# Expert order by rank, transposed network outputs and reordered norms in a two-block transformer kernel

## The reference

```python
proj = rms_norm(x, norm1_g) @ w_in              # 1024 x 3600
mq, mk, mv, mo, mi, mf, aq, ak, av = split(proj)
qk = silu(conv5(concat([mq, mk])))              # centred depthwise convolution over tokens
y_m = gated mLSTM of qk, mv, mo, mi, mf, both directions
y_a = dilated attention of rope(aq), rope(ak), av
x = x + concat([y_m, y_a]) @ w_out
u = relu(rms_norm(x, norm2_g) @ w_up)           # 1024 x 4096
x = x + (u * u) @ w_down
```

```python
x = layer_norm(ALPHA * x + h)                   # l0, l2
logits = x @ router                             # 8 experts, the best 2 of each token
for e in range(8):
    y = y + combine[:, e:e+1] * ((silu(g) * u) @ w_down[e])   # g, u = split(x @ w_gu[e]), 3584 wide
x = layer_norm(ALPHA * x + y)                   # l1, l3
```

## Time and profile before

| | |
|---|---|
| median of three runs | 2263.12 us |
| the profiled execution | 2262.86 us |
| its span, first to last instruction | 2261.0 us |
| PE, DVE, ACT busy share of the span | 95%, 71%, 58% |

### The profile page before, as it was taken

How to read it: one execution, slowest core, us unless ns; L and a number is a source line. 1 busy time by engine, 2 the same in 40 slices (tenths; PEclk the granted TensorE clock), 3 DMA queues, 4 the chain that set the end, 5 groups by cost and what they waited for, 6 DMA issues and landing times.

```text
span 2261.0 us, 26000 instructions
## 1 busy us (share of the span) xinstructions
PE 2140.9 (95%) x10012; PEld 1723.4 (76%) x10012; DVE 1601.9 (71%) x1566; ACT 1319.2 (58%) x1378; POOL 20.4 (1%) x32
## 2 busy tenths in 40 slices
PE   8889999989999999999888999999999999999997
PEld 7767887767888788877667888788888877777775
DVE  5866555776555645566756555788888899999998
ACT  6454444644544443444544544576776788888876
POOL 0000000000000000000000000000000000000000
PEclk9999999999999999997899999999999999999999
DMA  6314443422654345442007554789898999999995
GB/s 265 140 47 172 187 186 132 177 94 75 251 186 185 141 182 191 159 144 75 1 19 280 205 218 180 271 343 350 331 372 331 365 361 421 390 421 377 421 383 247
DMA packets 74625, 524.29 MB, mean 232 GB/s; under 512 B 8736, under 2 KB 9184, under 8 KB 12160
## 3 DMA queue, kind: packets, MB, share of 16 engines
q1 hardware_dynamic: 71712, 511.64, 58.5%
q0 software_dynamic: 2784, 10.93, 1.4%
HBM read 521.48 MB, written 1.05 MB: 231 GB/s over the span
## 4 chain that ended last, share of the span: by engine, by line
PE 68%; DVE 19%; issue 5%; ACT 5%; DMA 3%; DVEq 0%; SPq 0%; ACTq 0%
PE psum L518 58%; DVE LO L509 10%; DMA ring<-in_experts 2%; ACT HI L501 2%; DVE AR L1585 1%; PE psum L1055 1%; PE psum L2460 1%; PE psum L904 1%; PE psum L1050 1%; PE psum L841 1%; PE psum L686 1%; PE psum L667 1%; PE psum L1977 1%; PE psum L2523 1%; DVE AR L858 1%
## 5 line engine op out<-in xcount | busy, mean ns | idle before, releaser
L509 DVE TENSOR_TENSOR LO<-ring,HI 128x2048 fp32r<-128x2048 f32 x379 | 850.5, 2258 | 391.1 <-ACT HI L501 388.9
L501 ACT ACTIVATE HI<-ring 128x2048 fp32r<-128x2048 f32 x379 | 712.7, 1887 | 350.7 <-PE psum L518 339.5
L518 PE MATMUL psum<-HI,XT 128*128 128x512 f32 (+1 forms) x3152 | 803.9, 393 | 20.1 <-issue 5.1
L518 PEld LDWEIGHTS psum<-HI,XT 128*128 128x128 f32 x3152 | 592.0, 191 | 162.6 <-DVE XT L702 10.6
L518 PE MATMUL psum<-LO,XT 128*128 128x512 f32 (+1 forms) x1856 | 507.5, 395 | 17.1 <-DVE LO L509 14.6
L518 PEld LDWEIGHTS psum<-LO,XT 128*128 128x128 f32 x1856 | 345.6, 190 | 112.7 <-DVE LO L509 44.5
L518 PE MATMUL psum<-HI,HTH 128*128 128x512 f32 x848 | 305.4, 401 | 6.8 <-DVE HTH L1107 6.8
L509 DVE TENSOR_TENSOR LO<-AR,HI 128x2048 fp32r<-128x2048 f32 x112 | 254.7, 2289 | 53.5 <-ACT HI L501 52.9
L501 ACT ACTIVATE HI<-AR 128x2048 fp32r<-128x2048 f32 x112 | 212.5, 1910 | 59.0 <-PE psum L518 57.1
L518 PE MATMUL psum<-LO,HTH 128*128 128x512 f32 x848 | 229.1, 392 | 0.0
L518 PE MATMUL psum<-HI,HTL 128*128 128x512 f32 x568 | 221.5, 390 | 0.0
(11 more groups left out here) (281 smaller groups left out, 1462.8 us busy)
## 6 DMA issues: line engine op xcount, KB each, us to landing
ring<-in_experts SPq DMA_DIRECT2D x224, 1024.0 KB, 6.7
ring<-in_dense SPq DMA_DIRECT2D x149, 1024.0 KB, 4.8
AR<-in_experts SPq DMA_DIRECT2D x112, 1024.0 KB, 6.9
bcs<-in_ln_g POOLq DMA_DIRECT2D x4, 512.0 KB, 4.5
bcs<-in_ln_b POOLq DMA_DIRECT2D x4, 512.0 KB, 5.1
bcs<-in_norm_g POOLq DMA_DIRECT2D x3, 512.0 KB, 3.9
cons<-in_cons POOLq DMA_DIRECT2D x1, 1317.0 KB, 8.0
X<-in_x SPq DMA_DIRECT2D x2, 512.0 KB, 3.9
```

The costliest lines, as they stand in the source:

```text
L501: e.activation(HI[:, h:h + m], slot(u), ACT.Copy).then_inc(*high.up(u))
L509: e.tensor_tensor(LO[:, h:h + m], slot(u), HI[:, h:h + m].bitcast(F32), ALU.subtract).then_inc(*low.up(u))
L518: ins = e.matmul(out_ap, lhsT=a, rhs=b, start=start and n == 0, stop=stop and n == len(pairs) - 1)
```

## The change

Five things change. First, `SEATS` puts the experts in the order of ranks 0, 4, 1, 5, 2, 6, 3, 7; the tables KINDS, `thr` and the permutation follow it. Second, in ff0 and ff1 the chunks 1 to 7 are made transposed by `across`: the weights of the array are 128 columns of the unit, and the 256 tokens stream through. So the 8 transposes of such a chunk are gone, and ACT and DVE make HTH and HTL from SBUF. Third, part 1 (mk) of the front is made by `across` too, its transposes and its first eviction are gone. Fourth, in l2 `cols_lo` of tile 0 comes after the centred rows of tile 1. Fifth, in l3 the sum, mean and centring of tile 1 come before the last rows of tile 0.

```diff
+SEATS = [0, 4, 1, 5, 2, 6, 3, 7]
...
+    limits = [192.5, 128.5, 128.5, 999.0, 64.5, 64.5, 64.5, 999.0]
+    add("thr", np.tile(np.array(limits)[SEATS], (P, 1)))
+    add("seats", np.tile(np.array(SEATS), (P, 1)))
...
+        def across(e, use, key, x_ready):
+            for b in range(2):
+                banks.take(e, *use, b)
+            n = units[place[(*key, 0)]][0]
+            us = next_units(e, (*key, 0), KB // n)
+            for i, u in enumerate(us):
+                hv, lv = hi_lo(u)
+                last = i == len(us) - 1
+                for t in range(2):
+                    for w in x_ready(t, n * (i + 1) - 1):
+                        e.wait_ge(*w)
+                e.wait_ge(*high.of(u))
+                for b in range(2):
+                    for j in range(2):
+                        products(e, banks.get(*use, b)[:, j * S:j * S + S],
+                                 [(hv[:, k, tile(b * 2 + j)], z[:, i * n + k, :]) for k in range(n)
+                                  for z in (XTH, XTL)], i == 0 and j == 0, False)
+                e.wait_ge(*low.of(u))
+                for b in range(2):
+                    for j in range(2):
+                        ins = products(e, banks.get(*use, b)[:, j * S:j * S + S],
+                                       [(lv[:, k, tile(b * 2 + j)], XTH[:, i * n + k, :])
+                                        for k in range(n)], False, last and j == 1)
...
+        def still(c, gated):
+
+            return c >= 1 and not gated
+
         def net_up_tensor(e, use, key, c, kinds, gated, ready, swap, tile1=None):
+            if still(c, gated):
+                return across(e, (use, "up", c), (key, "up", c), ready)
...
+            if still(c, gated):
+                for b in range(2):
+                    e.wait_ge(*v_done.of(use, "gate", c, b))
+                    if c >= 2:
+                        e.wait_ge(*filled.of(use, "downed", c - 2))
+                    e.wait_ge(*a_order.last)
+                    e.activation(HTH[:, hb, 2 * b:2 * b + 2, :],
+                                 GS[:, hb, b, :].rearrange("p (j s) -> p j s", j=2),
+                                 ACT.Copy).then_inc(*a_done.up(use, "turn", c, b))
+                return between()
...
-            cols(e, ("raw", l, 1), ("qk", l, 1), BOTH, xr)
+            across(e, ("raw", l, 1), ("qk", l, 1), xr)
             few(e, ("gates", l), ("gates", l), xr)
-            pad_tensor(e, l, 0)
+            pad_tensor(e, l)
             cols(e, ("mv", l), ("mv", l), BOTH, xr,
                  mid={0: lambda: few_turn(e, ("gates", l), ("gates", l))})
-            pad_tensor(e, l, 1)
...
-                evict(e, ("raw", l, 1), t, raw[1][:, t, :])
+            pad_across(e, l)
...
-            pad_scalar(e, l, 1)
...
+        KINDS = [[kinds[r] for r in SEATS] for kinds in KINDS]
+        WIDTH = [[sum(kind) for kind in kinds] for kinds in KINDS]
...
-            e.tensor_tensor(PERM, bc3(RANK, 8, 1), bc3(idx, 8, 2), ALU.is_equal).then_inc(*v_done.up())
+            e.tensor_tensor(PERM, bc3(RANK, 8, 1), bc3(C("seats"), 8, 2),
+                            ALU.is_equal).then_inc(*v_done.up())
...
-                ln_apply(e, "l2", t, *vector("l2"), *vector("l2b"))
-                if t == 0:
+                ln_mean(e, "l2", t)
+                ln_center(e, t, *vector("l2"))
+                if t:
                     cols_lo(e, "l2", 0)
+                ln_sum(e, "l2", t)
+                ln_rows(e, "l2", t, *vector("l2b"))
...
-                ln_apply(e, "l3", t, *vector("l3"), *vector("l3b"))
+                ln_mean(e, "l3", t)
+                if t:
+                    ln_sum(e, "l3", 0)
+                ln_center(e, t, *vector("l3"))
+            for t in range(2):
+                if t == 0:
+                    ln_sum(e, "l3", 1)
+                ln_rows(e, "l3", t, *vector("l3b"))
```

More of the change, by code:

```diff
@@ L577, in cols_by_tile @@
                     between()
+        def across(e, use, key, x_ready):
[21 more added lines that the diff above has]
+                                        for k in range(n)], False, last and j == 1)
+                    if b:
+                        ins.then_inc(*used.up(u))
+                        if last:
+                            filled.tell((*use, b), used, u)
+                    elif last:
+                        ins.then_inc(*filled.up(*use, b))
         def row_part(e, use, t, u, i, kb, hb, first, stop, kinds, h_ready):
@@ L1010, in net_up_scalar @@
                 if c >= 2:
-                    e.wait_ge(*filled.of(use, "turn", c - 2, len(kinds) - 1))
+                    if still(c - 2, gated):
+                        e.wait_ge(*v_done.of(use, "turn", c - 2, t))
+                    else:
+                        e.wait_ge(*filled.of(use, "turn", c - 2, len(kinds) - 1))
                 e.wait_ge(*a_order.last)
@@ L1056, in net_turn_tensor, with net_turn_scalar @@
                 ins.then_inc(*filled.up(use, "turn", c, t))
[L1058 removed]
+        def net_turn_scalar(e, use, c, n, kinds, between, gated=True):
             hb, nb = c % 2, n // P
+            if still(c, gated):
+                for b in range(2):
[7 more added lines that the diff above has]
+                return between()
             for t, kind in enumerate(kinds):
@@ L1082, in net_turn_scalar, with net_turn_vector @@
                              ACT.Copy).then_inc(*a_done.up(use, "turn", c, t))
-        def net_turn_vector(e, use, c, n, kinds, between):
+        def net_turn_vector(e, use, c, n, kinds, between, gated=True):
             hb, nb = c % 2, n // P
+            if still(c, gated):
+                for b in range(2):
+                    xh = HTH[:, hb, 2 * b:2 * b + 2, :]
+                    e.wait_ge(*a_done.of(use, "turn", c, b))
+                    e.wait_ge(*v_order.last)
+                    e.tensor_tensor(HTL[:, hb, 2 * b:2 * b + 2, :],
+                                    GS[:, hb, b, :].rearrange("p (j s) -> p j s", j=2),
+                                    xh.bitcast(F32), ALU.subtract).then_inc(
+                        *v_done.up(use, "turn", c, b))
+                return between()
             for t, kind in enumerate(kinds):
@@ L1108, in net_turn_vector, with net_down_tensor @@
                                 ALU.subtract).then_inc(*v_done.up(use, "low", c, t))
-        def net_down_tensor(e, use, key, c, last, acc, kinds):
-            ready = [(v_bank if kind == P else v_done).of(use, "turn" if kind == P else "low", c, t)
-                     for t, kind in enumerate(kinds)]
+        def net_down_tensor(e, use, key, c, last, acc, kinds, gated):
+            ready = [(v_done if still(c, gated) or kind != P else v_bank).of(
+                use, "turn" if kind == P else "low", c, t) for t, kind in enumerate(kinds)]
             n = 0
```

85 lines of the change are left out of this document (56 added, 29 removed).

## The result

The changed kernel takes 2267.72 us (median of 19 runs, 2262.98 to 2276.85) against 2263.45 us (19 runs, 2258.34 to 2273.44) for the kernel before: ratio 1.0024, 95% interval 1.0013 to 1.0035. The forecast was 2250.5 us, with a range of 2243.5 to 2258.5. So the kernel is slower by 0.24%: the interval leaves out 1, but the change is smaller than the 0.5% that the prediction took as the least that can be told from no change. The median is 9 us beyond the range. Of the rivals only the third and fourth pointed up, and neither happened.

What follows compares the result with a forecast made beforehand. PE was taken to bound most of the kernel, the HI and LO chain the light experts, with DMA close behind. Terms -6.5 - 3.8 + 1.2 - 1.8 - 0.5 - 1.0 = -12.4 us gave 2250.5 us, range 2243.5 to 2258.5.

Steps and rivals of the forecast that it cites:

- third: Rival: in the networks and fronts, weight loads of 191 ns bound PE with 256-column matmuls; about 2359 us, chance 0.02.
- fourth: Rival: the limits meet the wrong ranks in the new expert order, so the other side runs; about 2528 us, chance 0.01.
- The order, -6.5 forecast: Experts: light ones all following heavy ones give -8.4, dearer fetches +1.5, heavy ones +0.4; between -8.4 and 0 us.
- 2.8 us a light expert: Experts: a light one after a heavy one takes 108.0 us, after a light one mean 110.8; three more gain 8.4.
- the sixth unit: Heavy experts: PE needs it at about 13.6 us; DVE ends its LO at 12.9 after heavy, 12.1 after light.
- the dearer fetch: Light experts: three now fetch 128 tokens for the next instead of 64, which costs 1.5 us back on DVE.
- the low end, nothing: Heavy experts following light ones: lower bound of their added cost, nothing; high end 6.9 us, 0.4 us taken.
- The networks, -3.8: ff0 and ff1: removed transposes give -12.5 us, 256-column matmuls cost +8.7; net -3.8 us.
- The fronts, +1.2: Front of each layer: part 1 by across costs PE +0.62 us, removed transposes give nothing; between -0.5 and +1.5.
- l2, -1.8 and -0.5: Norm l2: tile 1's last rows start 1.8 us earlier; the shorter PE gap gives the router's clock another 0.5 us.
- l3, -1.0: Norm l3: with tile 1's centring before tile 0's last rows, the end comes at 2257.5 us, -1.0 us.
- the signs that the prediction named as wrong: Profile: a heavy expert over 129 us, light ones still at 111, or pairs of matmuls away from 0.120.

Runs made afterwards that it cites:

- old places: The changed kernel with par at 232 columns instead of 144, so later tensors keep the addresses of the kernel before: 2254.18 us, ratio 0.9974.
- all but the order: The changed kernel with the old order of experts and the tensor addresses of the kernel before (par 232): 2255.52 us, ratio 0.9975.
- before again: The kernel before, unchanged, run once more for a trace: 2258.96 us in a single run.
- AR moved: The kernel before with EPS declared behind AR, so TMP2, TG and AR move by 32 bytes: 2255.99 us in a single run.
- order alone: The kernel before with only the new order of experts, tensors at the addresses of before (par 232): 2256.72 us, ratio 0.9981.
- right LO moved: Changed kernel at old places; in light experts' last turn but one, DVE makes the hidden rows' low part before LO: 2248.02 us, ratio 0.9934.

## Why the prediction was wrong

**The step that failed** is the price of the matmuls that don't change. The prediction took 0.227 us for 512 columns from the earlier trace rows, and by adding up its steps on the time of before it kept that pace for the changed kernel: the move of the tensors has no term in the sum, which puts it at nothing, without a reason. With XT, HTH and HTL moved by 352 bytes, the pace of 512 columns in the dense layers is 0.233. At one clock that costs 16.9 us, more than all that the change gains there (8.9): the kernel after is 7.8 us slower than before (2265.3 against some 2257.5). -12.4 + 16.9 would be +4.5 us, beside the 4.3 us measured between the medians. That closeness is luck: the real gain at old places was 8.9 us and not 12.4, and the 19 runs of before, of which only one has its clock on record, have a median of 2263.45 us, where its other sets have 2259.28 to 2262.36.

The same 0.227 was a misreading for the heavy experts. The prediction made 2.72 us of it for a unit; with XT it is 12 x 0.233 = 2.80, and the sixth unit is wanted at 14.0 us and not 13.6. No term hangs on it.

**The order, -6.5 forecast.** Direction right, size 1.7 times too large: -3.8 at one clock by itself, and -3.1 as what the full change gains (-8.9) less what all but the order gains (-5.8). The mis-sized term is the 2.8 us a light expert. It came from 108.0 against 111.2 and 110.4 us in the earlier trace rows, and the clock column of the same rows says 1.00, 0.98 and 0.98. About 2 us of it was the fall of the clock behind the wait for DVE, not the lead that a heavy expert leaves. The kernel before, profiled again without falls there, has 107.9, 108.7 and 108.9:

```profile
1805.50:1913.40 107.90, 101.30 (x491) 79.43 (x490) 101.11 (x66) 91.28 (x75) 0.00 (x0) 1.00 0.97 388
1913.40:2022.10 108.70, 101.99 (x492) 79.31 (x491) 102.63 (x67) 91.87 (x76) 0.00 (x0) 1.00 0.99 406
2022.10:2131.00 108.90, 101.87 (x491) 79.27 (x490) 102.58 (x67) 92.09 (x76) 0.00 (x0) 1.00 1.00 405
```

The lead is worth 0.9 us. Where no fall comes, three light experts together take 325.5 and 325.1 us in the old order (before again, AR moved) and 323.9 in the new (order alone, right LO moved). That is -1.4 with the dearer fetch in it, where the prediction had 329.6 to 3 x 108.5, -4.1. The last one, at a like clock of 0.97, takes 108.0 and 108.7 in the old order and 107.0 in the new, some -1.3 for the forecast's -2.8. These leave about 1 us of the -3.8 unread. The heavy experts behind light ones took 126.8 to 127.2 us at old places, where before had 126.9 to 127.3, so the low end, nothing, was right there.

**The networks, -3.8.** Right. From DVE's LO at 212.9 us to the one at 395.8, through ff0, the kernel after at old places and the one without the new order both gain 2.1 us against the second profile of before. From 568.7 to 735.4, through ff1, both gain 1.6. That is -3.7.

**The fronts, +1.2.** Right for layer 0: LO is 0.6 us later behind the products of part 1, in all kernels at old places with the edit. In after the convolution starts at 50.25 instead of 48.99, 1.3 later where 0.6 was forecast; 0.3 of that is there at the first LO already and 0.2 more by the fourth, before the edit. The transposes that are gone gave nothing back, as forecast. Layer 1's front lies among falls of the clock and can't be read.

**l2, -1.8 and -0.5.** Right: between the LO at 1063.7 us and at 1183.4 the kernels at old places gain 2.1 to 2.4 us in four profiles of six, against 2.3 forecast (of the other two, one loses 0.8 and one gains 3.7; the one that loses has a clock of 0.72 in the first 40 us of that stretch, where before has 0.83). In after, tile 1's last rows follow tile 0's by 7.28 us, where they followed by 8.84 in the earlier trace rows; `cols_lo` lies where it was put:

```profile
1174.13 1.54 DVE L851 SCALAR_TENSOR_TENSOR X<-AR,SML,bcs 128x512 f32<-128x512 f32 x2
...
1179.10 1.49 DVE L739 TENSOR_TENSOR XT<-psum,XT 128x512 fp32r<-128x512 f32 x2
...
1181.41 1.54 DVE L851 SCALAR_TENSOR_TENSOR X<-AR,SML,bcs 128x512 f32<-128x512 f32 x2
```

The router's stretch, 0.65 in the earlier trace rows, is at a full clock:

```profile
1184.00:1188.00 4.00, 3.54 (x29) 2.28 (x27) 3.37 (x4) 3.02 (x5) 0.29 (x1) 1.00 0.81 264
```

**l3, -1.0.** Right. The first residual lies 11.0 us before the end of the last rows, against 11.9 in the earlier trace rows and 10.9 forecast:

```profile
2249.88 0.69 DVE L2915 SCALAR_TENSOR_TENSOR X<-AR,psum 128x512 f32<-128x512 f32 x1 [3.36 <-PE psum L2668]
...
2259.37 1.54 DVE L851 SCALAR_TENSOR_TENSOR X<-AR,SML,bcs 128x512 f32<-128x512 f32 x2
```

So the networks, l2 and l3 came within some 0.3 us of their forecasts, and so did all but the order together (-5.8 for -5.9); the fronts can be read for one layer only. The sum missed because the pace under it moved. Of the signs that the prediction named as wrong, one appeared (matmuls of 256 columns away from 0.120, at 0.117 to 0.118), and I had not asked what could bring it.

## What to carry to other kernels

Read a diff for tensors that grow or shrink, also where no instruction uses the difference: everything allocated behind them moves, and with it the pace of matmuls can. Before comparing two versions in which PE is the bound, put both operands of the long products at the same place within 128 bytes, and read the pace by stage: one stage's 0.227 us was another's 0.233 in the same kernel. And before two stretches are subtracted, compare their clock columns; a wait of PE that costs nothing by itself can cost through the fall of the clock behind it. Taking it away pays then; filling it must not take longer than the wait.

## What the runs showed of the hardware

- Weights and stream of an fp32r matmul of 512 columns with 128 x 128 weights that lie side by side: 226.7 ns from start to start when their SBUF addresses differ by a multiple of 128 bytes, some 229 when they differ by 64 more, 231 to 238 by 32 or 96 more. With weights that are every second number: 233 to 234 at a difference of 0 and of 32. For 256 columns with x streaming: 119.9 to 120.7, and 117.3 to 118.3 at 32, 118.3 to 119.2 at 96.
- A clock of 1.2 GHz for 5 to 13 matmuls of 512 columns (427 ns each) came in light experts behind gaps of 1.4 to 2.5 us on PE, in 30 cases of 60, in some executions and not in others of the same kernel. The granted clock, by such falls there and elsewhere, is the main part of the spread of the runs: 2246.5 to 2263.6 us for the kernel after at old places goes with granted clocks of 0.976 and lower, down to 0.968.
- A matmul of 512 columns in fp32 (not fp32r), without use, shows as two records 0.43 us apart; three of them held PE for 2.6 us.
